# Means on VectorE and a reordered first split at the norms of a GLA and MLA decoder trunk

## The chip, the cores and the metric

The kernel runs on one core of one Trainium2 chip. The metric is the device time of one execution in microseconds (us), taken as the median over runs. Engines are named as in the profile: PE is TensorE (PEld its weight loads), DVE is VectorE, ACT is ScalarE, POOL is GpSimd, SP is SyncE, whose queue issues nearly all DMAs.

## The reference

Two decoder layers on x of 256 tokens by 2048 channels, in float32. Layer 0 is gated linear attention (GLA), layer 1 multi-head latent attention (MLA); each is followed by a gated MLP with a causal convolution of width 3. Every norm is an RMSNorm, modulated by a shift and a scale that come from the condition c; every residual is gated.

```python
def rmsnorm(x, g):
    xf = x.astype(jnp.float32)
    y = xf * lax.rsqrt(jnp.mean(xf * xf, axis=-1, keepdims=True) + EPS)
    return (y * g.astype(jnp.float32)).astype(x.dtype)

def modulate(h, shift, scale):
    return h * (1 + scale[:, None, :]) + shift[:, None, :]

# each layer:
    mod = c_act @ mod_w[i] + mod_b[i]          # 2048 by 12288 weights, six parts
    h = modulate(rmsnorm(x, norm_mix_g[i]), sh_m, sc_m)
    y = gla_mixer(h, ...) or mla_attention(h, ...)
    x = x + (1 + g_m)[:, None, :] * y
    h = modulate(rmsnorm(x, norm_ffn_g[i]), sh_f, sc_f)
    x = x + (1 + g_f)[:, None, :] * conv_ffn(h, w_up, conv_w, conv_b, w_down)
# at the end: rmsnorm(x, final_norm_g)
```

## The kernel before

**Weights as items.** All weight matrices are streamed as a numbered list of items of 4 row tiles by 512 columns (1 MB; the down projection of the last block group has 3 row tiles). SP loads item n into one of four buffers once PE has used item n-4. Float32 products are made from split numbers: ACT copies an item to its rounded high part (`hi`, L764), DVE subtracts to get the low part (`lo`, L1213), and PE multiplies high by high, high by low and low by high. `item` (L1893) has three orders: the plain one multiplies all high parts first (L1911, L1912) and the low parts last (L1918); the one with `turn` or `halves` (L1903 to L1905) needs the low part from its start. The last item of a section that ends in a norm has `halves`: the first 128 tokens are finished before the others. `AHEAD` is 3: ACT and DVE split item n+3 while PE multiplies item n.

**Modulation tiles.** The vector c times its 2048 by 2048 parts is made on DVE: one tile of 128 rows (1 MB) at a time is loaded into one of two buffers `mods` and gathered into `acc` (L1230). `MOD_PLACES` (L437) says at which item of which section each tile is gathered; SP issues its load three items ahead (L629 to L646), in the sections `gla_out` to `norm1` after the item's load, and waits for the gather of the tile two before (L551). A finished vector is summed over partitions by PE: `reduce_mod` (L1977) makes 16 products of one column for parts 4, 10 and 12 (L1990), and DVE adds the bias and makes the scale columns in `reduced` (L1276; L1293, L1295).

**A section before a norm.** `add_section` on DVE (L1382) handles the GLA output projection: per item it runs `lo`, the gather of `mods_at` and, for each finished chunk of 512 columns, gate times output plus x (L1350, L1351). `add_last` (L1353) does the last chunk in two token halves: L1357 and L1358 after the first half (`half_used`), L1360 and L1362 after the item (`item_used`). ACT squares each chunk and accumulates it along the row (L796), so that four partial sums for each of the two token tiles stand in `sq`. Here DVE gathers a modulation tile at items 3 to 14 of `gla_out`.

**The norm itself.** POOL's `boundary_root` (L698) adds the first three partial sums (L702, L703), and after the last squares the fourth (L705), makes mean plus epsilon (L706) and raises it to -0.5 (L707). While POOL does so, DVE makes the low part of item 14 + 3 of the section (L1395, L1733, L1872) and, before norm1 and norm5, the scale columns (`reduced(4)`, `reduced(12)`). Then DVE normalises the first two chunks (L1370), ACT the others later (L819). PE transposes xn in 8 fills of two channel tiles (16 fills at norm2, for two modulations), L1954, into the two banks of `tp`. Each fill is split: ACT makes the rounded modulated high part straight from the bank (L779), then DVE makes the modulated value (L1322) and subtracts (L1327). The first fill is handled tile by tile on DVE, so that PE can begin when the first tile's low part is there (`first_lo`, L2029). `turn_boundary` (DVE L1373, ACT L822) and `turn_two` (L1764, L844) hold this order; before fills 4 and 6 (at norm2 before every even fill from 4) DVE also makes the low parts of the next items.

The norms of this form are norm1 (after `gla_out`), norm2 (after `down02`), norm5 (after `mla_out`) and final. norm3 and norm4 are norms of the two latents, 512 wide; their sums come from ACT (L788) and their root from POOL (`root`, L688; L692 the mean, L693 the power). norm3's result is applied by DVE at fill 14 of norm2 (L1773), norm4's at L1789. At the end `scale_output(3)` (L1880, L1757) multiplies the last chunk by the final gain, and L1886 and L1194 apply the root.

Each engine executes its own instructions in order; they meet at semaphores.

Of the kernel before, what the change touches and what calls it, by code (L numbers as in the profile page):

```python
# [21 lines left out]
ALU = mybir.AluOpType  # L22
# [9 lines left out]
AHEAD = 3  # L32
# [104 lines left out]
def yoco_kernel(nc, x, c, positions, mod_w, mod_b, norm_mix_g, norm_ffn_g, gla_w_in, gla_w_gate2,  # L137
# [173 lines left out]
    with ExitStack() as ctx:  # L311
# [38 lines left out]
        half_used = sem("half_used")  # L350
        first_lo = sem("first_lo")
# [80 lines left out]
        def taken(m):  # L432
# [7 lines left out]
            ("gla_out", 4, 4, tuple(range(3, 15))),  # L440
# [25 lines left out]
        SUMS = {"norm0": 1, "norm3": 2, "norm4": 3}  # L466
        NORM = {"norm0": 0, "norm1": 1, "norm2": 2, "norm3": 3, "norm4": 4, "norm5": 5, "final": 6}
# [197 lines left out]
        def _(pool):  # L665
# [70 lines left out]
            boundary_root("norm1")  # L736
            boundary_root("norm2")
            norm_root("norm3", LAT)
            norm_root("norm4", LAT)
# [7 lines left out]
            boundary_root("norm5")  # L747
            boundary_root("final")
# [3 lines left out]
        def _(act):  # L752
# [19 lines left out]
            def split(fill, count, dst, scale, shift, from_=0):  # L772

                for f in range(count):
# [7 lines left out]
                    ins.then_inc(split_hi, 1)  # L782

# [38 lines left out]
            def turn_boundary(name, next_item, dst, scale, shift):  # L822

                s = a[name]
                for f in range(8):
# [4 lines left out]
                    split(s.tp + f, 1, dst, scale, shift, f)  # L830
# [13 lines left out]
            def turn_two(next_item):  # L844
# [3 lines left out]
                for f in range(16):  # L848
# [8 lines left out]
                    if f < 8:  # L857
                        split(s.tp + f, 1, (a_hi,), (kv,), (ab[:, A_OF["kv"] + 1],), f)
# [344 lines left out]
        def _(dve):  # L1203
# [102 lines left out]

            def split(name, count, dst, hi_of, scale, shift, from_=0, wrap=KT, both=both):

                fill = a[name].tp
                for f in range(from_, from_ + count):  # L1310

                    dve.wait_ge(split_hi, splits[name] + f + 1)
                    first = name in BOUND and f == 0
                    for ks in ((0,), (1,)) if first else ((0, 1),):
                        for m, (d, h_, sc_, sh_) in enumerate(zip(dst, hi_of, scale, shift)):
                            for k in ks:
                                kt = 2 * (f % wrap) + k
                                t = tp[:, (fill + f) % 2, k * T:(k + 1) * T]
                                if sh_ is None:
                                    ins = dve.tensor_scalar(both[:, k, :], t, sc_[:, kt:kt + 1], None, ALU.mult)  # L1320
                                else:
                                    ins = dve.tensor_scalar(both[:, k, :], t, sc_[:, kt:kt + 1],  # L1322
                                                            sh_[:, kt:kt + 1], ALU.mult, ALU.add)
                                v = step.mark(ins)
                            step.wait(v)
                            kts = slice(2 * (f % wrap) + ks[0], 2 * (f % wrap) + ks[-1] + 1)
                            ins = dve.tensor_tensor(d[:, kts, :], both[:, ks[0]:ks[-1] + 1, :],  # L1327
                                                    h_[:, kts, :].bitcast(F32), ALU.subtract)
# [44 lines left out]
            def turn_boundary(name, next_item, dst, hi_of, scale, shift):  # L1373
# [3 lines left out]
                for f in range(8):  # L1377
                    if f in (4, 6):
                        lo(next_item + f // 2)
# [1096 lines left out]
```

## Time and profile before

| | us |
|---|---|
| median of 3 runs | 2393.55 |
| lowest, highest | 2393.10, 2397.02 |
| the profiled execution: its time | 2393.17 |
| its span in the profile | 2391.2 |
| PE busy | 2308.2 |
| PEld busy | 1870.2 |
| DVE busy | 1847.2 |
| ACT busy | 1096.9 |
| POOL busy | 126.6 |

The span runs from the first to the last instruction of the profile; the execution's own time is 2.0 us longer. Busy times are of one engine each and overlap. A busy PE is not a PE at its peak: the mean granted clock was 0.982 of full speed, and it is below 1 just in a few stretches.

### The profile page before, as it was taken

To read this page: it belongs to the slowest core of one execution; us is meant where nothing else is said; L and a number is where in the kernel's file an instruction comes from. 1 tells how busy PE (TensorE), PEld (TensorE's weight loads), DVE (VectorE), ACT (ScalarE), POOL (GpSimd) and SP (SyncE) were. 2 spreads that over 40 slices of the span, in tenths; PEclk is the share of its full clock that TensorE was granted. 3 is DMA by queue.
4 is the path that set the end of the run, shared out by engine and by line. 5 is a ranking of instruction groups with operands and counts; after the bars stand their busy time and mean duration, and the time that the engine had idled before them with its cause. 6 is when DMAs were issued, how large, how long until landed. Compare 5 with 4: busy or idle time off the path is not lost.

```text
span 2391.2 us, 26862 instructions
## 1 busy us (share of the span) xinstructions
PE 2308.2 (97%) x10800; PEld 1870.2 (78%) x10800; DVE 1847.2 (77%) x1748; ACT 1096.9 (46%) x1192; POOL 126.6 (5%) x145
## 2 busy tenths in 40 slices
PE   5999999999999999999998999999999999999998
PEld 2478887778887888878887788877887888878886
DVE  5868997887998888888888777887777556564565
ACT  2244443544554354533554555435555345444454
POOL 0021740010000000000000000000000000000000
PEclk8999999999999999999999999999999999999999
DMA  9958789787997998889889475696776555555554
GB/s 363 383 198 293 250 300 351 250 315 268 348 325 275 359 336 304 291 303 370 323 281 330 130 224 187 253 340 218 274 270 223 193 194 178 190 177 193 193 180 154
DMA packets 259807, 632.89 MB, mean 265 GB/s; under 512 B 23505, under 2 KB 32745, under 8 KB 233978
## 3 DMA queue, kind: packets, MB, share of 16 engines
q1 hardware_dynamic: 258050, 625.90, 73.8%
q10 hardware_dynamic: 1656, 5.60, 0.6%
q8 instruction: 69, 1.13, 0.2%
q14 instruction: 32, 0.26, 0.0%
HBM read 629.36 MB, written 2.10 MB: 264 GB/s over the span
## 4 chain that ended last, share of the span: by engine, by line
PE 80%; DVE 8%; DMA 5%; issue 3%; ACT 2%; SPq 1%; POOL 1%; DVEq 0%; POOLq 0%; ACTq 0%
PE gm L1911 22%; PE gm L1912 22%; PE gm L1918 22%; PE tp L1954 2%; PE gm L1903 2%; DMA mods<-in_mod_w_dram 2%; PE gm L1905 2%; PE gm L1904 2%; DVE w_lo L1213 1%; DVE acc L1230 1%; DVE conv L1659 1%; DMA raw<-in_ffn_w_down_dram 1%; ACT w_hi L764 1%; PE ms L2064 1%; DMA raw<-in_gla_w_in_dram 1%
## 5 line engine op out<-in xcount | busy, mean ns | idle before, releaser
L1213 DVE TENSOR_TENSOR w_lo<-raw,w_hi 128x2048 fp32r<-128x2048 f32 (+1 forms) x378 | 851.9, 2255 | 330.2 <-ACT w_hi L764 328.5
L764 ACT ACTIVATE w_hi<-raw 128x2048 fp32r<-128x2048 f32 (+1 forms) x378 | 703.8, 1864 | 695.5 <-DMA raw<-in_ffn_w_up_dram 242.2
L1911 PE MATMUL gm<-w_hi,h_hi 128*128 128x512 f32 x1816 | 720.7, 397 | 1.6 <-DVE h_lo L1327 1.6
L1912 PE MATMUL gm<-w_hi,h_lo 128*128 128x512 f32 x1816 | 708.1, 390 | 0.0
L1918 PE MATMUL gm<-w_lo,h_hi 128*128 128x512 f32 x1816 | 448.7, 389 | 0.0
L1230 DVE SCALAR_TENSOR_TENSOR acc<-mods,c_col,acc 128x2048 f32<-128x2048 f32 x180 | 422.7, 2349 | 5.3 <-DMA mods<-in_mod_w_dram 4.8
L1911 PEld LDWEIGHTS gm<-w_hi,h_hi 128*128 128x128 f32 x1816 | 341.2, 188 | 77.9 <-issue 4.7
L1918 PEld LDWEIGHTS gm<-w_lo,h_hi 128*128 128x128 f32 x1816 | 340.9, 188 | 70.7
L1912 PEld LDWEIGHTS gm<-w_hi,h_lo 128*128 128x128 f32 x1816 | 341.3, 188 | 69.9 <-issue 1.7
L1911 PE MATMUL gm<-w_hi,a_hi 128*128 128x512 f32 x692 | 275.1, 398 | 11.6 <-DVE a_lo L1682 8.1
L1912 PE MATMUL gm<-w_hi,a_lo 128*128 128x512 f32 x692 | 271.2, 392 | 0.0
L1659 DVE SCALAR_TENSOR_TENSOR conv<-tp,cv_col,conv 128x255 f32<-128x255 f32 (+1 forms) x352 | 152.4, 477 | 76.9 <-ACT conv L1026 73.5
L1918 PE MATMUL gm<-w_lo,a_hi 128*128 128x512 f32 x692 | 173.4, 391 | 0.0
L1911 PEld LDWEIGHTS gm<-w_hi,a_hi 128*128 128x128 f32 x692 | 131.0, 189 | 43.6 <-DVE a_lo L1682 10.4
L1912 PEld LDWEIGHTS gm<-w_hi,a_lo 128*128 128x128 f32 x692 | 130.9, 189 | 28.4 <-issue 1.4
L1918 PEld LDWEIGHTS gm<-w_lo,a_hi 128*128 128x128 f32 x692 | 129.0, 188 | 26.2
L1026 ACT ACTIVATE conv<-tp,cv_col 128x256 f32<-128x256 f32 x176 | 88.4, 561 | 120.7 <-PE tp L1954 120.3
L770 ACT ACTIVATE u<-gm 128x1024 f32<-128x1024 f32 x76 | 77.5, 1020 | 133.3 <-PE gm L1918 129.6
L702 POOL TENSOR_TENSOR sq<-sq 128x2 f32<-128x2 f32 x4 | 5.3, 1329 | 1832.1 <-ACT tp L796 1832.1
L733 POOL TENSOR_TENSOR ex<-ex,qk_t 128x512 f32<-128x512 f32 x32 | 78.5, 2474 | 106.3 <-ACT ex L937 106.3
L1039 ACT ACTIVATE a_hi<-gated 128x256 f32 (+1 forms) x88 | 35.7, 417 | 85.7 <-DVE gated L1674 85.7
L779 ACT ACTIVATE h_hi<-tp,ab 128x256 fp32r<-128x256 f32 x64 | 32.0, 563 | 87.4 <-DVE ab L1445 50.9
(267 smaller groups left out, 2155.0 us busy)
## 6 DMA issues: line engine op xcount, KB each, us to landing
raw<-in_ffn_w_up_dram SPq DMA_DIRECT2D x176, 1024.0 KB, 5.1
mods<-in_mod_w_dram SPq DMA_DIRECT2D x170, 1024.0 KB, 7.1
raw<-in_ffn_w_down_dram SPq DMA_DIRECT2D x64, 1024.0 KB, 5.1
raw<-in_gla_w_in_dram SPq DMA_DIRECT2D x48, 1024.0 KB, 5.2
mods<-in_kv_mod_w_dram SPq DMA_DIRECT2D x32, 1024.0 KB, 7.0
raw<-in_ffn_w_down_dram SPq DMA_DIRECT2D x32, 768.0 KB, 4.4
raw<-in_gla_w_o_dram SPq DMA_DIRECT2D x16, 1024.0 KB, 7.1
raw<-in_mla_w_o_dram SPq DMA_DIRECT2D x16, 1024.0 KB, 5.6
```

Of the source, the lines that this page charges most:

```text
L733: pool.tensor_tensor(f, f, s, ALU.mult).then_inc(xq_made, 1)
L764: act.activation(w_hi[:, k % RAW, 0:words], raw[:, k % RAW, 0:words], ACT.Copy).then_inc(hi_made, 1)
L770: act.activation(dst, gm[:, par] if src is None else src, func).then_inc(u_made, 1)
L1026: ins = act.activation(conv[:, j % 2, side, :], tp[:, bank, side * T:(side + 1) * T], ACT.Identity, scale=cv_col[:, layer, 2, cs], bias=cv ...
L1213: dve.tensor_tensor(w_lo[:, k % RAW, 0:words], raw[:, k % RAW, 0:words], w_hi[:, k % RAW, 0:words].bitcast(F32), ALU.subtract).then_inc(lo ...
L1230: return dve.scalar_tensor_tensor(total, tile_, ck, total, ALU.mult, ALU.add)
L1659: ins = dve.scalar_tensor_tensor(v, tp[:, bank, side * T:(side + 1) * T - shift], cv_col[:, layer, tap, cs], v, ALU.mult, ALU.add)
L1903: pe.matmul(o, hi_s[:, kt, tok], wh[:, j, :], start=kt == 0, stop=False)
L1904: pe.matmul(o, hi_s[:, kt, tok], wl[:, j, :], start=False, stop=False)
L1911: pe.matmul(o, hi_s[:, kt, tok], wh[:, j, :], start=kt == 0, stop=False)
L1912: pe.matmul(o, lo_s[:, kt, tok], wh[:, j, :], start=False, stop=False)
L1918: return pe.matmul(o, hi_s[:, kt, tok], wl[:, j, :], start=False, stop=kt == total - 1)
```

## The change

Four things. The partial sums and the mean of norm1 to norm5 and final move from POOL to DVE: `add_last` adds the first three sums between its two halves, `boundary_root` and `latent_root` make mean plus epsilon, and POOL keeps only the power (`mean_root`). The first fill of norm1, norm2 and norm5 is split in another order: DVE makes the modulated value in `both`, ACT copies it to the rounded high part, DVE subtracts. The low part of the item that DVE made after `add_last` is now made before fill 2, and `reduced` comes after the normalising. The modulation tiles of `gla_out` are gathered (and loaded) one item earlier.

```diff
-            ("gla_out", 4, 4, tuple(range(3, 15))),
+            ("gla_out", 4, 4, tuple(range(2, 14))),
...
+        MEAN = {"norm1": 0, "norm2": 1, "norm3": 2, "norm4": 3, "norm5": 4, "final": 5}
...
-            def boundary_root(name):
-
-                done, dst = 8 * BOUND[name], TT * (NORM[name] % 2)
-                pool.wait_ge(sq_made, done + 6)
-                step.link(pool.tensor_tensor(sq[:, 4, :], sq[:, 0, :], sq[:, 1, :], ALU.add))
-                step.link(pool.tensor_tensor(sq[:, 4, :], sq[:, 4, :], sq[:, 2, :], ALU.add))
-                pool.wait_ge(sq_made, done + 8)
-                step.link(pool.tensor_tensor(sq[:, 5, :], sq[:, 4, :], sq[:, 3, :], ALU.add))
-                step.link(pool.tensor_scalar(sq[:, 5, :], sq[:, 5, :], 1.0 / D, EPS, ALU.mult, ALU.add))
+            def mean_root(name):
+
+                dst = TT * (NORM[name] % 2)
+                pool.wait_ge(mean_made, MEAN[name] + 1)
                 pool.tensor_tensor(stats[:, 1, dst:dst + TT], sq[:, 5, :], half_neg[:, 0:TT],
                                    ALU.pow).then_inc(rstd, 1)
...
+            def first_split(name, dst):
+
+                for k in range(2):
+                    act.wait_ge(both_made, 2 * BOUND[name] + k + 1)
+                    ins = act.activation(dst[:, k, :], both[:, k, :], ACT.Copy)
+                    ins.then_inc(first_hi if k == 0 else split_hi, 1)
...
+            def first_split(name, dst, hi_of, scale, shift):
+
+                fill = a[name].tp
+                dve.wait_ge(tp_done, fill + 1)
+                for k in range(2):
+                    dve.tensor_scalar(both[:, k, :], tp[:, fill % 2, k * T:(k + 1) * T], scale[:, k:k + 1],
+                                      shift[:, k:k + 1], ALU.mult, ALU.add).then_inc(both_made, 1)
+                dve.wait_ge(first_hi, BOUND[name] + 1)
+                dve.tensor_tensor(dst[:, 0, :], both[:, 0, :], hi_of[:, 0, :].bitcast(F32),
+                                  ALU.subtract).then_inc(first_lo, 1)
+                dve.wait_ge(split_hi, splits[name] + 1)
+                dve.tensor_tensor(dst[:, 1, :], both[:, 1, :], hi_of[:, 1, :].bitcast(F32),
+                                  ALU.subtract).then_inc(tp_free, 1)
+                dve.wait_ge(first_lo, BOUND[name] + 1)
+                dve.wait_ge(tp_free, fill + 1)
...
                 dve.tensor_tensor(x_sb[:, 0, cols], x_sb[:, 0, cols], u[:, 1, 0], ALU.add).then_inc(x_half, 1)
+                dve.wait_ge(sq_made, 8 * BOUND[after] + 6)
+                step.link(dve.tensor_tensor(sq[:, 4, :], sq[:, 0, :], sq[:, 1, :], ALU.add))
+                step.link(dve.tensor_tensor(sq[:, 4, :], sq[:, 4, :], sq[:, 2, :], ALU.add))
                 dve.wait_ge(item_used, a[name].item + 16)
...
+            def root(name, total, width):
+
+                dve.tensor_scalar(sq[:, 5, :], total, 1.0 / width, EPS, ALU.mult, ALU.add).then_inc(mean_made, 1)
+
+            def boundary_root(name):
+
+                dve.wait_ge(sq_made, 8 * BOUND[name] + 8)
+                step.link(dve.tensor_tensor(sq[:, 4, :], sq[:, 4, :], sq[:, 3, :], ALU.add))
+                root(name, sq[:, 4, :], D)
+
+            def latent_root(name):
+
+                dve.wait_ge(sums, TT * SUMS[name])
+                k = TT * (NORM[name] % 2)
+                root(name, stats[:, 0, k:k + TT], LAT)
...
-            def turn_boundary(name, next_item, dst, hi_of, scale, shift):
-
+            def turn_boundary(name, next_item, dst, hi_of, scale, shift, columns):
+
+                boundary_root(name)
                 dve.wait_ge(rstd, NORM[name] + 1)
                 normalise_chunks(name)
+                reduced(columns)
                 for f in range(8):
-                    if f in (4, 6):
+                    if f in (2, 4, 6):
                         lo(next_item + f // 2)
+                    if f == 0:
+                        first_split(name, dst[0], hi_of[0], scale[0], shift[0])
+                        continue
                     split(name, 1, dst, hi_of, scale, shift, f)
...
                 add_last(name, after)
-                lo(s.item + AHEAD + 14)
...
             def turn_two(next_item):
 
+                boundary_root("norm2")
                 dve.wait_ge(rstd, NORM["norm2"] + 1)
                 normalise_chunks("norm2")
...
-                    if f >= 4 and f % 2 == 0:
+                    if f >= 2 and f % 2 == 0:
                         lo(next_item + f // 2)
                     if f == 14:
+                        latent_root("norm3")
                         normalised("norm3", lat[:, 0], lat[:, 0], TT)
...
             lo(m.item)
+            latent_root("norm4")
             normalised("norm4", lat[:, 1], lat[:, 1], TT)
...
             add_last("mla_out", "norm5")
-            lo(s.item + AHEAD + 14)
-            reduced(12)
...
+            boundary_root("final")
             scale_output(3)
             dve.wait_ge(y_scaled, 4)
             dve.wait_ge(rstd, NORM["final"] + 1)
```

The general `split` on DVE loses its case for the first fill, and `down02` loses its `lo` after `add_last` in the same way as the other two.

## Rows read from the trace of the kernel before

**Rows 1.** The page, engines' shares of the chain that ended last:
```profile
PE 80%; DVE 8%; DMA 5%; issue 3%; ACT 2%; SPq 1%; POOL 1%; DVEq 0%; POOLq 0%; ACTq 0%
```

**Rows 2.** Waits of PE over the whole span: us in total, times, longest:
```profile
PE tp L1954 <- DVE xn L1370: 6.4, 3, 3.1
...
PE ms L1990 <- DVE acc L1230: 2.3, 1, 2.3
```

**Rows 3.** Timeline of DVE, end of `gla_out`: start, us, instruction, idle before:
```profile
521.21 2.34 DVE L1230 SCALAR_TENSOR_TENSOR acc<-mods,c_col,acc 128x2048 f32<-128x2048 f32 x1
525.22 2.35 DVE L1230 SCALAR_TENSOR_TENSOR acc<-mods,c_col,acc 128x2048 f32<-128x2048 f32 x1 [1.67 <-DMA mods<-in_mod_w_dram]
...
530.14 2.28 DVE L1213 TENSOR_TENSOR w_lo<-raw,w_hi 128x2048 fp32r<-128x2048 f32 x1
```

**Rows 4.** Timeline of ACT and POOL, the root of norm1:
```profile
530.79 0.19 ACT L796 ACTIVATION_READ_ACCUMULATOR tp<-x_sb 128x1 f32 x1
531.13 1.35 POOL L705 TENSOR_TENSOR sq<-sq 128x2 f32<-128x2 f32 x1 [7.53 <-ACT tp L796]
...
532.84 0.69 POOL L707 TENSOR_TENSOR stats<-sq,half_neg 128x2 f32<-128x2 f32 x1
```

**Rows 5.** The chain that ended last, in order of time, around norm1: start, us, what:
```profile
527.62 5.68 PE ms L1990 x32
...
533.75 0.89 DVE xn L1370 x2
...
534.89 1.10 PE tp L1954 x4
...
537.71 0.44 DVE h_lo L1327
...
538.19 0.79 PE gm L1903
```

**Rows 6.** Timelines of DVE and SP's queue, start of `gla_out`:
```profile
460.97 2.29 DVE L1213 TENSOR_TENSOR w_lo<-raw,w_hi 128x2048 fp32r<-128x2048 f32 x1 [2.58 <-ACT w_hi L764]
...
451.71 0.50 SPq L553 DMA_DIRECT2D mods<-in_mod_w_dram  x1
```

**Rows 7.** Stretches at norm1 and norm5: busy shares, then granted clock (PEclk), DMA:
```profile
542.00:543.00 1.00, 1.00 (x4) 0.76 (x4) 0.00 (x0) 0.99 (x2) 0.00 (x0) 0.63 0.00 0
...
1631.00:1632.00 1.00, 1.00 (x7) 0.96 (x6) 0.00 (x0) 0.09 (x1) 0.00 (x0) 0.70 0.00 0
```

**Rows 8.** Tiles `gated` and `stats`, small operations: duration min/median/max in ns:
```profile
L1039 ACT ACTIVATE a_hi<-gated x88: 401/418/423, 604.2 to 2329.6; 128x256 f32 x48, 128x256 fp32r<-128x256 f32 x40
...
L1827 DVE TENSOR_SCALAR stats<-stats x16: 169/170/170, 1423.0 to 1545.5; 128x2 f32<-128x2 f32 x16
```

**Rows 9.** Timelines of DVE at norm2 and norm5, and of PE at norm5:
```profile
1313.96 0.68 DVE L1360 TENSOR_TENSOR u<-gm,gate_b 128x512 f32<-128x512 f32 x1
...
1618.96 0.69 DVE L1360 TENSOR_TENSOR u<-gm,gate_b 128x512 f32<-128x512 f32 x1 [1.16 <-PE gm L1905]
...
1618.76 4.44 PE L1990 MATMUL ms<-ones,acc 128*128 128x1 f32 x32
...
1628.23 0.80 PE L1903 MATMUL gm<-w_hi,h_hi 128*128 128x512 f32 x1 [1.35 <-DVE h_lo L1327]
```

**Rows 10.** Timeline at fills 2 and 14 (DVE) and norm3's power (POOL):
```profile
543.13 0.99 DVE L1322 TENSOR_SCALAR both<-tp,ab 128x256 f32<-128x256 f32 x2 [2.33 <-ACT h_hi L779]
...
1367.78 0.88 DVE L1343 TENSOR_SCALAR lat<-lat,stats 128x512 f32<-128x512 f32 x2
...
1359.27 2.74 POOL L693 TENSOR_TENSOR stats<-stats,half_neg 128x2 f32<-128x2 f32 x1
```

**Rows 11.** Timeline of PE at fill 14, and of DVE and POOL at the end:
```profile
1370.43 0.47 PE L1903 MATMUL gm<-w_hi,h_hi 128*128 128x512 f32 x1
...
2381.01 1.23 DVE L1757 TENSOR_TENSOR y_out<-x_sb,mods 128x1024 f32<-128x1024 f32 x1
...
2381.80 0.49 POOL L705 TENSOR_TENSOR sq<-sq 128x2 f32<-128x2 f32 x1 [8.66 <-ACT tp L796]
```

More of the change, by code:

```diff
@@ L735, in _ @@
                 root(TT * h, TT, DV, o_sums, TT * (h + 1), o_rstd)
[L736 to L739, printed above, removed]
+            mean_root("norm1")
+            mean_root("norm2")
+            mean_root("norm3")
+            mean_root("norm4")
             pool.wait_ge(tp_free, at["norm4"].tp + 2)
@@ L746, in _ @@
                 step.mark(ins) if k == 0 else ins.then_inc(consts, 1)
-            boundary_root("norm5")
-            boundary_root("final")
+            mean_root("norm5")
+            mean_root("final")
         @block.scalar
@@ L829, in turn_boundary @@
                         hi(next_item + AHEAD)
-                    split(s.tp + f, 1, dst, scale, shift, f)
+                    if f == 0:
+                        first_split(name, dst[0])
+                    else:
+                        split(s.tp + f, 1, dst, scale, shift, f)
             def latent_out(side):
@@ L857, in turn_two @@
                     if f < 8:
-                        split(s.tp + f, 1, (a_hi,), (kv,), (ab[:, A_OF["kv"] + 1],), f)
+                        if f == 0:
+                            first_split("norm2", a_hi)
+                        else:
+                            split(s.tp + f, 1, (a_hi,), (kv,), (ab[:, A_OF["kv"] + 1],), f)
                     else:
@@ L1312, in split @@
                     dve.wait_ge(split_hi, splits[name] + f + 1)
[L1313 to L1328, printed above, removed]
-                            if m < len(dst) - 1:
-                                step.link(ins)
-                            elif first and ks == (0,):
-                                ins.then_inc(first_lo, 1)
-                            else:
-                                ins.then_inc(tp_free, 1)
@@ new lines, in split @@
+                    for m, (d, h_, sc_, sh_) in enumerate(zip(dst, hi_of, scale, shift)):
+                        for k in range(2):
+                            kt = 2 * (f % wrap) + k
+                            t = tp[:, (fill + f) % 2, k * T:(k + 1) * T]
+                            if sh_ is None:
+                                ins = dve.tensor_scalar(both[:, k, :], t, sc_[:, kt:kt + 1], None, ALU.mult)
+                            else:
+                                ins = dve.tensor_scalar(both[:, k, :], t, sc_[:, kt:kt + 1],
+                                                        sh_[:, kt:kt + 1], ALU.mult, ALU.add)
+                            v = step.mark(ins)
+                        step.wait(v)
+                        kts = slice(2 * (f % wrap), 2 * (f % wrap) + 2)
+                        ins = dve.tensor_tensor(d[:, kts, :], both[:, :, :], h_[:, kts, :].bitcast(F32), ALU.subtract)
+                        if m < len(dst) - 1:
+                            step.link(ins)
+                        else:
+                            ins.then_inc(tp_free, 1)
@@ L1644, in _ @@
             add_section("gla_out", "norm1")
[L1645 removed]
             turn_boundary("norm1", a["up00"].item, (h_lo,), (h_hi,), (ab[:, A_OF["ffn0"]],),
[L1647 removed]
+                          (ab[:, A_OF["ffn0"] + 1],), 4)
             def conv_tile(layer, g, blk, j, fill, tile_):
```

14 lines of the change are left out of this document (9 added, 5 removed).

## The prediction

> **What bounds the kernel now.** I read the chain that ended last, then PE's waits, then the timelines of each stretch that the diff touches. In the chain PE holds 80% of the span, DVE 8% and POOL 1% [rows 1]. So almost everywhere a step off PE costs nothing, and the change can only act where PE stands still. The waits name these places: 6.4 us in three waits for xn, which are norm1, norm2 and norm5, and 2.3 us before the reduction of part 4 [rows 2]. Around each norm PE has no work until the first low part is there: at norm1 its item ends at 527.62 - 2.33 = 525.3, and its next large product starts at 538.19 [rows 2, 5]. I follow that stretch backwards, because each instruction in it is one that the change moves.
>
> At norm1 DVE is late before the norm starts. Its gather of item 13 ends at 523.55, and then it waits 1.67 us for the last tile, gathers until 527.57 and only then begins with the last chunk [rows 3]. PE's reduction also waits for that gather and takes 5.68 us [rows 5]. After the last squares (530.98) POOL needs until 533.53 [rows 4]. Of this the fourth addition takes 1.35 us on two numbers a partition. It ends at 532.48, and DVE's low part of a whole item (530.14 + 2.28) ends at 532.42 [rows 3, 4]. At the end of the kernel it is the same again: DVE's product ends at 2382.24, POOL's addition, 0.49 us this time, at 2382.29 [rows 11]. So POOL stands until DVE's operation on two SBUF tiles is over. A page of the Trainium skill, "SBUF — State Buffer", section "Who interferes with whom", says so: DVE instructions with two SBUF inputs exclude a GpSimd instruction that reads SBUF, and the first to issue keeps the port. By that rule, the trace agrees.
>
> **Gathers one item earlier.** DVE's idle 2.58 us before item 3's low part [rows 6] takes the extra gather (2.34 us) at item 2. Its tile comes early enough: the first load was issued at 451.71, after item 6's load; one item earlier it goes out at about 445, some 13 us before its gather at 458.4, and SP passes the next weight load no later, since the gather of two tiles before is long done. From item 3 on all gathers stand where they stood, and the one at item 14 is gone. The cover for this is that 2.58 us; without it DVE would be 2.3 us late on low parts that PE does not wait for in that section. So L1357 starts at 523.6 instead of at about 527.5. Its two operations and the two new sums (0.17 us each by the small DVE operation [rows 8], 0.21 with the link) end at 525.4, when PE's item has just ended. L1360 and L1362 then end at 526.85, and the squares at 527.6 instead of 530.98: **3.4 us**.
>
> **The mean on DVE, the lo moved.** From the end of the squares to the start of xn POOL took 2.58 us (2.77 at norm1 with `reduced` behind it) [rows 4, 5]. After: 0.06 handoff, 0.21 sum, 0.17 mean, 0.06 handoff, 0.69 power [rows 4, 8], 0.03 handoff = 1.22 us. DVE has nothing running meanwhile, so POOL does not stand. That is **1.4 us** at each of norm1, norm2 and norm5. At norm1 xn starts at 528.8, and PE can transpose 1.14 us later, at 529.95, as it did after 533.75 [rows 5]. PE must also have finished the reduction, which now starts at 525.3. It took 4.44 us at norm5, right behind full work [rows 9], and 5.68 us here, so it ends between 529.7 and 531.0. I take the 4.44, since it will be as at norm5; the upper bound costs 1.0 us. `reduced` behind xn ends at 530.9, before the transposes of the first fill (531.1), so it costs nothing; with a 5.68 us reduction it would also end before its fill does.
>
> The additions inside `add_last` are free where DVE waits for PE after L1358, as at norm5 (1.16 us idle). At norm2 L1360 followed without idle time [rows 9], so there they cost **0.4 us**. They wait for the third chunk's squares, which end before L1358 does at all four norms; behind that wait stands the last chunk.
>
> The moved low part (2.28 us) falls before fill 2, where DVE was idle for 2.33 us [rows 10]. PE wants that item only after 24 products of the first one, over 8 us after its start, so I cost it at nothing; without cover it is 2.2 us a norm.
>
> **The first split.** From the transposes' end (534.89 + 1.10) to PE's product it took 2.20 us [rows 5]. After: 0.06 handoff, 0.54 the modulated value (0.99 for two [rows 10]), 0.03, ACT's copy 0.42 [rows 8], 0.03, subtraction 0.44 [rows 5], 0.05 = 1.57 us. The second value (done 0.99 after the start) and the second copy lie beside. **0.6 us** at each of three norms. The copy reads SBUF in the row and here alike.
>
> **norm3 and norm4.** Before, POOL had norm3's root ready by 1362.0, long before DVE used it at 1367.78 [rows 10]. Now DVE makes the mean at that place and waits: 0.17 + 0.06 + 0.69 + 0.04 = 0.96 us. What is queued behind is fill 14's low part, and PE waited for just that: its product stands at 1370.43, right behind it [rows 11]. So this **costs 1.0 us**, the whole of it. At norm4 the mean stands behind a low part for which PE waits and ahead of nothing that PE waits for, so nothing.
>
> **The end.** `boundary_root("final")` stands before `scale_output(3)`, which used to run (2381.01) while ACT squared [rows 11]. Now DVE waits for the squares until 2381.7, makes sum and mean until 2382.1 and starts the 1.23 us product 0.03 us later, ahead of POOL, which the handoff delays by 0.06. POOL stands until 2383.35; norm3's power shows what follows: it started under a DVE low part, took 2.74 us and ended 0.55 us after that was over [rows 10]. So the root comes at 2383.9 instead of 2383.35: **0.5 us lost**. If POOL were not held, the product would end at 2383.35 and nothing would be lost. The same section of "SBUF — State Buffer" in the Trainium skill gives the port to whoever issues first; had POOL been first, by its 0.69 us the product would end at about 2384.1, 0.7 us lost.
>
> **The sum.** norm1: 538.19 - (529.95 + 1.14 + 1.57) = 5.5 us. norm2: 1.4 + 0.6 - 0.4 = 1.6. norm5: 1.4 + 0.6 = 2.0; its squares end 2.2 us after L1360's start as at norm1, at 1621.1, so the transposes can start at 1621.1 + 1.22 + 1.14 = 1623.5, and the reduction is over at 1623.2 [rows 9]. Less 1.0 (norm3) and 0.5 (end): 7.6 us. Against the profiled execution (2393.17) this is 2385.6; the median of the runs shown is 0.4 us above it, so **2386.0 us**. What comes later keeps the gain, because loads and splits are paced by the items that PE has used.
>
> The clock is the term that I set at zero. PE's clock is at 1.2 GHz when it starts after a norm (granted 0.50) and returned to 2.4 GHz at 542.7, 4.5 us after the first product, and at norm5 at 1631.6, 3.4 us after it (1628.23) [rows 5, 7, 9]; where in its slice it returned follows from the slice's mean, 0.63 and 0.70. At half the clock each us costs about 0.5. I assume that the return moves with the start. If it comes 1.1 us earlier or later, as these two rows differ, at all three norms, that is 1.7 us either way.
>
> **The rivals.** (a) The clock's return does not move with the start. Then half of the 9.1 us by which the starts move is lost at the lower clock: 4.6 - 1.5 = 3.1 us gained, **2390.5**. For it: in the rows the return does not stand at a fixed distance from the start. (b) The last tile of part 4 is late all the same, for its load is paced by gathers, not by items (it waited 1.67 us [rows 3]). Then norm1 gains just 1.8 us: 3.9 us in all, **2389.7**. Against it: the load of item 13's tile came in time before, with one more tile behind it. (c) The moved low part delays fill 2 at three norms: 3 x 2.2 lost, 1.0 us gained, **2392.6**. Against it stands DVE's idle time of that length. (d) Slower: POOL's long first operations are a start after idle time and do not come from DVE's operation beside them. Then the power, now POOL's only operation, meets it each time. At 2.74 us [rows 10] it costs 2.05 more at norm1, norm2, norm3, norm5 and final: 10.3 lost against 7.6, **2396.2**. It turns the sign when the power takes over 0.69 + 1.5 = 2.2 us at each. Against it: the two ends within 0.06 us of DVE's, and the 0.69 us of the powers with DVE idle. (e) That the gathers do not move or the root still waits for POOL's sums is excluded by the diff.
>
> **How the numbers follow.** Forecast 0.76, (a) 0.09, (b) 0.06, (c) 0.05, (d) 0.04. A measurement can tell 0.2% (4.8 us) from no change. Faster by more: nearly all of the forecast, 0.75. Within: the rest of it, (a) to (c) and most of (d), 0.22. Slower by more: 0.03. The range: at the low end the clock gives 1.7 us, the end loses nothing (0.5), and 0.3 is left for the handoffs, 2386.0 - 2.5 = 2383.5; at the top it reaches (a) with its 2390.5, which also holds the forecast less 1.0 for the longer reduction and 1.7 for the clock.
>
> **What would show it.** Right: L1357 of norm1 at about 523.6 without a gather before it; 1.2 us from the squares' end to xn; powers of 0.69 us, except one of 1.7 at the end; first products after the norms 5.5, 1.6 and 2.0 us sooner after their section's last product; a PE wait of 1 us at fill 14. Wrong: a power above 1 us at norm1, norm2 or norm5; idle PE before item 1 of `up00` or `latent`; a clock that returns over 6 us after the first product; PE waiting in `gla_out` for low parts.

## The result and the profile after

The changed kernel took 2382.31 us in the median of 5 executions (2379.17 to 2385.29) against 2393.1 for the kernel before (5 executions): ratio 0.9947, interval 0.9934 to 0.9959. The profiled execution took 2379.23 us with a span of 2377.1. The forecast was 2386.0 with a range from 2383.5, so the direction was right and the gain came out larger than the range allowed.

At norm1 the order of the steps is the predicted one. In the chain that ended last, around norm1 of the changed kernel (start, us, what):

```profile
520.25 2.35 DVE acc L1242
522.60 0.61 DVE u L1380
...
524.23 0.70 DVE u L1386
...
526.43 0.17 DVE sq L1397
...
526.63 0.18 DVE sq L1392
...
526.88 0.70 POOL stats L706
...
527.60 0.89 DVE xn L1412 x2
...
528.74 1.10 PE tp L2003 x4
...
529.94 0.55 DVE both L1324
...
530.58 0.42 ACT h_hi L787
...
531.03 0.44 DVE h_lo L1327
...
531.51 0.79 PE gm L1952
```

The last gather is followed by the last chunk without a wait [rows 3 had 1.67 us]. From the last square (526.41) to xn (527.60) it is 1.19 us, where the prediction had 1.22. From the transposes' end (529.84) to the product (531.51) it is 1.67, for 1.57. What is not the predicted one is where the last chunk lies against PE (PE's timeline):

```profile
522.89 4.61 PE L2039 MATMUL ms<-ones,acc 128*128 128x1 f32 x32
```

PE's item ends at 522.89, where the reduction begins without a wait. The first half of the chunk (L1380) starts 0.4 us before that, where the prediction had 1.7 (523.6 against 525.3), and the second half (L1386) 1.34 us after it, where the prediction had 0.1 (525.4). So the gap that the prediction saw after the change was 7.8 us (13.3 less 5.5), and this profile has 8.9.

The PE waits of the same profile (us in total, times, longest) show the three waits for xn at 4.3 us instead of 6.4 [rows 2]:

```profile
PE tp L2003 <- DVE xn L1412: 4.3, 3, 2.2
```

POOL's power over the whole run (ns min/median/max):

```profile
L706 POOL TENSOR_TENSOR stats<-sq,half_neg x6: 690/691/1612, 526.9 to 2367.7; 128x2 f32<-128x2 f32 x6
```

Five take 0.69 us, norm3's among them (2.74 before [rows 10]). The long one is at the end, in the timeline of the end (start, us, instruction, idle before):

```profile
2367.44 0.17 DVE L1392 TENSOR_SCALAR sq<-sq 128x2 f32<-128x2 f32 x1
2367.52 1.22 DVE L1801 TENSOR_TENSOR y_out<-x_sb,mods 128x1024 f32<-128x1024 f32 x1
2367.69 1.61 POOL L706 TENSOR_TENSOR stats<-sq,half_neg 128x2 f32<-128x2 f32 x1 [758.34 <-DVE sq L1392]
```

DVE's product is issued first and ends at 2368.74, the power 0.56 us after that. At norm3 and fill 14 the cost stands where it was forecast (timelines of POOL, DVE and PE):

```profile
1354.59 0.69 POOL L706 TENSOR_TENSOR stats<-sq,half_neg 128x2 f32<-128x2 f32 x1 [48.20 <-DVE sq L1392]
1355.32 0.88 DVE L1366 TENSOR_SCALAR lat<-lat,stats 128x512 f32<-128x512 f32 x2 [0.81 <-POOL stats L706]
...
1357.98 0.47 PE L1952 MATMUL gm<-w_hi,h_hi 128*128 128x512 f32 x1 [0.97 <-DVE h_lo L1353]
```

So in these two profiles the single steps have nearly their sizes, norm1 as a whole gains 4.4 us for 5.5, and together they do not give 10.8 us. Matching the two traces product by product gives 14.1 us of span: 4.4 at norm1, 1.5 at norm2, 1.2 at norm5, less 1.0 and 0.5; the other 8.4 us came in stretches that the change does not touch. One is a clock fall. From 1018 to 1030 us the granted clock was 0.72 in the kernel before and 1.00 in its repeat (first `before`, then r1_before; stretch, PE, PEld, DVE, ACT, POOL busy, then granted clock, DMA share, GB/s):

```profile
1018.00:1030.00 12.00, 9.29 (x32) 7.21 (x31) 6.06 (x7) 2.58 (x4) 0.00 (x0) 0.72 0.49 175
```
```profile
1018.00:1030.00 12.00, 10.15 (x47) 8.41 (x48) 6.06 (x8) 5.38 (x5) 0.00 (x0) 1.00 0.73 268
```

Where the rest of the 8.4 us came from is not shown. Two theories follow: (A) the change is worth its own terms, the rest is the chance of few executions; (B) the 10.8 us are its lasting worth. Repeats and part changes had to tell them apart.

### The profile page after: what moved, and what is told of

Read it like the earlier page. It is cut to its first block, busy times and chain, and to the rows that moved or that the text cites. A ratio compares the mean times of both kernels' runs of the same rounds, so it can differ in the third digit from the quotient of the medians.

```text
span 2377.1 us, 26862 instructions
## 1 busy us (share of the span) xinstructions
PE 2301.8 (97%) x10800; PEld 1865.5 (78%) x10800; DVE 1849.8 (78%) x1766; ACT 1096.3 (46%) x1192; POOL 111.3 (5%) x127
## 4 chain that ended last, share of the span: by engine, by line
PE 49%; issue 34%; DVE 8%; DMA 5%; ACT 2%; SPq 1%; POOL 0%; POOLq 0%; DVEq 0%; ACTq 0%
PE gm L1960 12%; PE gm L1961 12%; PE gm L1967 12%; DVE acc L1242 2%; PE tp L2003 2%; DVE w_lo L1225 2%; DMA mods<-in_mod_w_dram 1%; PE gm L1952 1%; ACT w_hi L763 1%; PE gm L1954 1%; PE gm L1953 1%; PE ms L2113 1%; DMA raw<-in_ffn_w_down_dram 1%; PE ms L2247 1%; DMA raw<-in_mla_w_o_dram 1%
## 5 line engine op out<-in xcount | busy, mean ns | idle before, releaser
L1960 PEld LDWEIGHTS gm<-w_hi,a_hi 128*128 128x128 f32 x692 | 129.9, 188 | 42.9 <-DVE a_lo L1727 10.3
L706 POOL TENSOR_TENSOR stats<-sq,half_neg 128x2 f32<-128x2 f32 x6 | 5.1, 844 | 1919.7 <-DVE sq L1392 1919.7
```

What stands on the lines that cost most here:

```text
L1960: pe.matmul(o, hi_s[:, kt, tok], wh[:, j, :], start=kt == 0, stop=False)
```

## The experiments

The yardstick is the gap: from the start of the section's last product to the start of the first product after the norm (at norm1 of the kernel before 524.90 to 538.19, of the changed one 522.66 to 531.51). Loads and clock outside it do not touch it; a clock that falls inside it does. The last column runs from the start of the last product of all to the end of the span.

| profile of | norm1 | norm2 | norm5 | end |
|---|---|---|---|---|
| before | 13.3 | 10.3 | 9.7 | 12.1 |
| r1_before | 15.6 | 9.6 | 9.7 | 12.2 |
| r3_before | 17.1 | 9.6 | 9.7 | 12.1 |
| after | 8.9 | 8.8 | 8.5 | 12.6 |
| r2_after | 9.8 | 7.8 | 7.6 | 12.6 |
| e6_after_again | 8.0 | 9.3 | 7.8 | 12.6 |
| r4_after | 8.6 | 7.7 | 7.8 | 12.6 |
| e11_after_third | 9.5 | 7.7 | 8.5 | 12.6 |
| e1_only_gather | 10.1 | 9.6 | 9.7 | 12.1 |
| e9_gather_again | 9.7 | 9.8 | 9.7 | 12.1 |
| e2_no_gather | 12.2 | 8.4 | 7.4 | 12.6 |
| e7_only_lo | 16.6 | 8.5 | 9.1 | 12.1 |
| e8_only_split | 16.9 | 9.0 | 9.1 | 12.1 |
| e3_mean3_early | 8.7 | 8.1 | 7.4 | 12.6 |
| e4_root_late | 8.4 | 9.2 | 7.8 | 12.1 |
| e5_both | 8.7 | 9.7 | 7.8 | 12.1 |
| e10_both_again | 8.2 | 7.7 | 7.5 | 12.2 |

### The kernel before, again

No edit.

> The kernel before once more, unchanged, for a second profile and more times. Theory A (own steps): the change itself gains what the three gaps around norm1, norm2 and norm5 show, 4.4 + 1.5 + 1.2 us, less 1.0 at norm3 and 0.5 at the end, 5.6 us together; the other 8 us between the two profiles come from stalls outside the changed code at which the clock happened to fall in one execution and not in the other. Then this profile lies anywhere between 2388 and 2397, and its clock falls at other places than 1020.6 and 1433.6. Theory B (the rest is systematic): the stalls near 1020 and 1433 lower the clock in every execution of this kernel; then both low stretches, 6.8 and 3.4 us long, are here again.

Measured: 2389.76 us, ratio 0.9999 (0.9983 to 1.0014). Both theories miss here: the profiled execution took 2384.65 us, below theory A's 2388, and from 1018 to 1030 and from 1425 to 1445 us its granted clock was 1.00, where theory B wanted both low stretches again.

> The kernel before once more, for a third profile of it and one more session. Theory C (each term is near its size, but the kernel before varies more than the changed one, because its last tile at norm1 comes at a time that its load sets): the gap from the last product of gla_out to the first of up00 is anywhere from 13 to 17 us, against 8.0 to 9.8 in the changed kernel's three profiles; the gaps at norm2 and norm5 are 9.6 to 10.3 and 9.7 us; no stretch between the norms is longer than in the changed kernel by more than clock falls and landings explain. Rival D (something between the norms is lastingly slower in the kernel before): one such stretch is over 2 us longer with the same clock.

Measured: 2393.89 us, ratio 1.0004 (0.9993 to 1.0014). The gap at norm1 is 13.3, 15.6 and 17.1 us in the three profiles of one and the same kernel, with norm2 and norm5 alike. Theory C holds and D falls: its stretches between the norms are 772.0, 298.1 and 754.4 us long, the changed kernel's (r4_after, same session) 774.6, 299.4 and 753.1. The timelines of DVE and PE in r3_before show where the time is:

```profile
524.92 2.35 DVE L1230 SCALAR_TENSOR_TENSOR acc<-mods,c_col,acc 128x2048 f32<-128x2048 f32 x1 [2.63 <-DMA mods<-in_mod_w_dram]
...
527.33 1.01 PE L1990 MATMUL ms<-ones,acc 128*128 128x1 f32 x4 [4.83 <-DVE acc L1230]
```

and its stretches (columns as above):

```profile
527.30:534.30 7.00, 6.97 (x32) 6.90 (x32) 4.76 (x5) 3.25 (x5) 2.23 (x3) 0.50 0.21 82
534.30:538.00 3.70, 1.95 (x9) 1.57 (x8) 2.02 (x6) 0.88 (x2) 0.00 (x0) 0.50 0.00 0
```

The last tile came 2.63 us late, not 1.67, and the last gather began 2.4 us after PE's item had ended (527.33 - 4.83 = 522.50). In the profile that the prediction was read from it began 0.1 us before that (525.22 against 525.29). PE stood for 4.83 us instead of 2.33 [rows 2], and the reduction then ran wholly at 1.2 GHz: 7 us instead of 5.68 [rows 5].

In r1_before the last gather began 0.9 us after PE's item had ended (524.94 - 3.30 = 521.64):

```profile
522.53 2.35 DVE L1230 SCALAR_TENSOR_TENSOR acc<-mods,c_col,acc 128x2048 f32<-128x2048 f32 x1 [2.67 <-DMA mods<-in_mod_w_dram]
...
524.94 6.99 PE L1990 MATMUL ms<-ones,acc 128*128 128x1 f32 x32 [3.30 <-DVE acc L1230]
```

The issue of that tile's load, on SP's queue in `before`, r1_before and r3_before, says what differs:

```profile
519.11 0.34 SPq L553 DMA_DIRECT2D mods<-in_mod_w_dram  x1
```
```profile
515.10 0.34 SPq L553 DMA_DIRECT2D mods<-in_mod_w_dram  x1
```
```profile
517.85 0.34 SPq L553 DMA_DIRECT2D mods<-in_mod_w_dram  x1
```

Each time it goes out within 0.03 us of the end of the gather of item 12, which frees the buffer. From there to the last gather it is 6.1, 7.4 and 7.1 us, so this transfer was about 1 us quicker in the profile that the prediction was read from. And the issue came 6.2, 6.5 and 4.7 us before PE's item ended: in r3_before DVE itself was 1.5 us further behind PE.

### The changed kernel, again

No edit.

> The changed kernel once more. Theory A: low clock stretches may appear near 1012 and 1423, and the gain over the kernel before comes nearer to 5.6 us, a time of about 2387. Theory B: no low stretch there again, and a time within 2 us of 2381.

Measured: 2385.39 us, ratio 0.9976 (0.9964 to 0.9989), nearer to theory A's 2387 than to theory B's 2381. From 1418 to 1432 us its clock was low (granted 0.76).

> The changed kernel once more, in a third session. Theory A (own terms 5.6 us, the rest chance): a ratio of 0.9970 to 0.9985, as the 0.9976 of the second session. Theory B: a ratio of 0.9955 or less, as the 0.9947 of the first.

Measured: 2381.42 us, ratio 0.9948 (0.9928 to 0.9968): theory A missed, theory B's band met.

> The changed kernel once more, beside the kernel before of the same session. Theory C: in the mean 7 to 9 us less than the kernel before; ratio 0.9962 to 0.9972, and a smaller scatter than the kernel before has. Theory B (10.8 us and more is the change's lasting worth): 0.9955 or less.

Measured: 2385.12 us, ratio 0.9961 (0.9947 to 0.9974), just below C's band. The smaller scatter that C expected is not shown: all 42 executions of the changed kernel scatter by 3.4 us (standard deviation), 143 of the kernel before by 3.8.

> The changed kernel beside these two. Theory C: 8 to 9 us less than the kernel before (7.2 at norm1, 1.1 at norm2, 2.0 at norm5, less 1.0 at norm3 and 0.5 at the end), ratio 0.9962 to 0.9967; the gap at norm1 8 to 10 us, with at most 0.5 us of wait for the last tile.

Measured: 2383.21 us, ratio 0.9962 (0.9946 to 0.9977), as C expected.

In the means of the five sessions the change gained 11.2, 6.7, 12.6, 7.6 and 8.5 us; weighted by the executions of the changed kernel (5, 12, 6, 7, 12) that is 8.8 us (2392.8 to 2384.1). The gains of 6.7 and 12.6 us have standard errors of 1.2 and 1.6 us, so the sessions differ by somewhat more than their scatter explains. Each ran on another chip, as far as recorded (the first is not); what makes them differ stays open. If each execution counts alike, the 8.8 us have an error of 0.7, and neither A's 5.6 nor B's 10.8 stands. If each session counts alike, the gain is 9.3 with an error of 1.1: A still falls, B is not ruled out by the times. Against B stand the terms themselves, which add up to less.

### The gathers alone, and all but the gathers

```diff
# e1_only_gather, e9_gather_again: the kernel before with
-            ("gla_out", 4, 4, tuple(range(3, 15))),
+            ("gla_out", 4, 4, tuple(range(2, 14))),
# e2_no_gather: the changed kernel with
-            ("gla_out", 4, 4, tuple(range(2, 14))),
+            ("gla_out", 4, 4, tuple(range(3, 15))),
```

> The kernel before with the gathers of gla_out at items 2 to 13 and nothing else. Own steps: DVE begins the last chunk at about 523.5, the squares end 3.4 us sooner, the root follows at 2.58 us, xn at 530.3 instead of 533.75, and norm1's gap shrinks by about 3.2 us; 0.13% faster, about 2390. If the gap at norm1 does not shrink, the reduction of part 4 or the scale columns behind it bound it, and the time stays within 1 us of before.

Measured: 2388.42 us, ratio 0.9984 (0.9971 to 0.9998). The gap at norm1 is 10.1 us, the expected 3.2 less than in the profile of `before`.

> The kernel before with the gathers of part 4 one item earlier, once more. Theory C (the norm1 term was too small because the profile it was read from had an early last tile; without a gather at item 14 that lateness is gone, and with it the slow reduction behind it): no wait of DVE for the last tile, a reduction of at most 5.4 us, the gap at norm1 10 to 11 us against the 13.3, 15.6 and 17.1 us of the kernel before, so 5 to 6 us of gain from this one part where the prediction had 3.4 with the reduction's 1.2; norm2 and norm5 as before, 9.6 and 9.7 us. In the time 4 to 6 us, ratio 0.9975 to 0.9985. Rival E (the tile is late one item earlier as well, in some executions): a DVE wait of 1 us or more before the last gather, and a gap of 12 us or more.

Measured: 2387.78 us, ratio 0.9984 (0.9970 to 0.9997). The gap is 9.7 us, even under the 10 expected. Its PE timeline at the reduction and its stretch:

```profile
521.02 3.64 PE L1990 MATMUL ms<-ones,acc 128*128 128x1 f32 x32
```
```profile
521.10:524.60 3.50, 3.50 (x33) 3.47 (x31) 3.35 (x3) 1.93 (x3) 1.06 (x1) 0.98 0.60 190
```

PE did not stand before the reduction, kept its 2.4 GHz (granted 0.98) and took 3.64 us. Rival E falls: neither profile has a DVE wait there. With 15.3 us as the mean of the three gaps before, this part alone is worth 5.4 us at norm1 (15.3 to the mean of 10.1 and 9.7); the forecast had 3.4.

> The changed kernel with the gathers back at items 3 to 14. Own steps: norm1's gap is about 3 us longer than in the changed kernel, everything else as there: about 2385. If the gathers explain none of it, within 1 us of the changed kernel.

Measured: 2389.30 us, ratio 0.9991 (0.9977 to 1.0005), 4 us over the expected 2385. The gap at norm1 is 12.2 us, 3.2 over the mean of the changed kernel, so from this side the gathers are worth 3.2 us and from e1 and e9 5.4; each rests on one or two profiles. The late tile is back, with all the rest of the change in place (DVE's timeline):

```profile
523.10 2.35 DVE L1242 SCALAR_TENSOR_TENSOR acc<-mods,c_col,acc 128x2048 f32<-128x2048 f32 x1 [2.78 <-DMA mods<-in_mod_w_dram]
```

### The moved low part alone

```diff
 # turn_boundary
-                    if f in (4, 6):
+                    if f in (2, 4, 6):
                         lo(next_item + f // 2)
 # turn_two
-                    if f >= 4 and f % 2 == 0:
+                    if f >= 2 and f % 2 == 0:
 # behind add_last, twice
-                lo(s.item + AHEAD + 14)
```

> The kernel before, with one edit: the low part of the next section's first item goes from ahead of the norm to ahead of fill 2. POOL still makes the sums, the mean and the power. Theory A (POOL's fourth addition took 1.35 us because DVE's operation on two SBUF tiles held the port): that addition takes 0.2 us at norm1, norm2 and norm5, from the last square to xn it is 1.4 to 1.5 us rather than 2.6, and the gaps at norm2 and norm5 are 1.1 us shorter, 8.7 and 8.6 us; at norm1 the 5 to 7 us reduction still stands ahead of xn, so less is gained there. Rival (the sums on POOL are slow by themselves, for POOL has stood for hundreds of us): the addition stays at 1.3 us and the gaps at 9.7 us. If theory A holds, moving the mean to DVE as such is worth under 0.4 us a norm.

Measured: 2390.74 us, ratio 0.9987 (0.9975 to 0.9999). POOL's fourth addition, all four norms (ns min/median/max):

```profile
L705 POOL TENSOR_TENSOR sq<-sq x4: 194/194/484, 529.7 to 2381.8; 128x2 f32<-128x2 f32 x4
```

The addition falls from 1.35 [rows 4] to 0.19 us at the three norms, and stays at 0.48 at the end [rows 11], where DVE's product on two SBUF tiles still runs. A start after idle time, rival (d), is no cost. Norm2 gained the 1.1 us. Norm5 gained 0.6 only, for what was late next (timeline of ACT, POOL and DVE):

```profile
1621.10 0.19 ACT L796 ACTIVATION_READ_ACCUMULATOR tp<-x_sb 128x1 f32 x1
...
1621.98 0.69 POOL L707 TENSOR_TENSOR stats<-sq,half_neg 128x2 f32<-128x2 f32 x1
...
1622.89 0.17 DVE L1293 TENSOR_TENSOR modc<-ms,pcol 128x16 f32<-128x16 f32 x1 [2.36 <-PE ms L1987]
...
1623.30 1.67 DVE L1370 TENSOR_SCALAR xn<-x_sb,stats 128x512 f32<-128x512 f32 x4
```

The power ended at 1622.67, but `reduced` stood ahead of xn and waited for PE's reduction. That is what moving `reduced` behind xn is for; the prediction had counted its worth without naming it.

This run also says what the first of the four changes is worth. From the last square (1621.29) to the end of the power it is 1.38 us here, with sums and mean still on POOL, and 1.17 us in the changed kernel (526.41 to 527.58). So of the 1.4 us that the prediction gives to "the mean on DVE, the lo moved" about 1.2 come from the moved low part, and 0.2 from the mean on DVE. By the prediction's own terms the same move costs 0.4 us at norm2 and, where its wait was placed badly, 1.0 at norm3 and 0.5 at the end. The change without it was not run.

### The first split alone

```diff
+                    if f == 0:
+                        first_split(name, dst[0], hi_of[0], scale[0], shift[0])
+                        continue
                     split(name, 1, dst, hi_of, scale, shift, f)
```

and the same in `turn_two` and on ACT.

> The kernel before, with one edit: the first split goes from DVE to ACT to DVE. Theory A: from the end of the first fill's transposes to the first product 1.6 us rather than 2.2, so gaps 0.6 us shorter at each of norm1, norm2 and norm5 (9.1 us at norm5). Rival (the copy on ACT comes no sooner than the copy from PSUM did, and two handoffs are added): 2.1 us or more, gaps as before.

Measured: 2389.17 us, ratio 0.9989 (0.9977 to 1.0001). The gap at norm5 is 9.1 us, at norm2 9.0. In the timeline at norm5 the product starts 2.69 us after the first transpose does (1619.62 to 1622.31), where it was 3.30 at norm1 of the kernel before (534.89 to 538.19 [rows 5]), so 0.6 us less, as forecast. The time of the whole run (an interval that holds 1) shows nothing by itself:

```profile
1619.62 1.94 PE L1991 MATMUL tp<-ident,xn 128*128 128x128 f32 x8 [2.57 <-DVE xn L1401]
...
1620.75 0.99 DVE L1327 TENSOR_SCALAR both<-tp,ab 128x256 f32<-128x256 f32 x2 [0.59 <-PE tp L1991]
...
1622.31 0.80 PE L1940 MATMUL gm<-w_hi,h_hi 128*128 128x512 f32 x1 [0.75 <-DVE h_lo L1330]
```

### Mending the two losses

```diff
 # e3_mean3_early: the changed kernel with
-                    if f == 14:
+                    if f == 13:
                         latent_root("norm3")
+                    if f == 14:
 # e4_root_late: the changed kernel with
-            boundary_root("final")
             scale_output(3)
+            boundary_root("final")
 # e5_both, e10_both_again: both
```

> After, with norm3's mean moved from ahead of fill 14's low part to ahead of fill 13's. Theory A (the change is worth what its own terms add up to, norm3's mean costing 1.0 us because fill 14's low part stands behind DVE's wait for the power): the power runs beside a low part of fill 13, PE's wait at fill 14 of about 1 us goes away unless the mean's inputs are not there yet, and the time between the last product of norm2's side and fill 14's product is 0.9 to 1.0 us shorter. The power may then take up to 2.7 us beside DVE's operation without harm. Rival (the 0.96 us at norm3 came from something else, a load or the clock): the stretch between norm2 and norm5 keeps its length and PE waits as before. Whole time: 1 us less than after, not to be told from it by the median.

Measured: 2383.11 us, ratio 0.9953 (0.9935 to 0.9971). In the timeline at fill 14 neither DVE nor PE waits any more, and matched product by product the trace gains 1.00 us at that place. The power ran at fill 13, where DVE had no low part beside it, and took 0.69 us:

```profile
1356.12 0.87 DVE L1366 TENSOR_SCALAR lat<-lat,stats 128x512 f32<-128x512 f32 x2
...
1358.77 0.47 PE L1953 MATMUL gm<-w_hi,h_hi 128*128 128x512 f32 x1
```

> After, with the last tile's product with the scale put ahead of the final norm's sum and mean, as it was before the change. Theory A (at the end POOL's power is held by DVE's product on two SBUF tiles): the product starts about 0.9 us sooner, as before the change, and ends before the power can start; the power takes 0.69 us, not 1.61, and the stretch from PE's last product to the end is 0.4 to 1.0 us shorter than after's 12.59 us. Rival (the power at the end is slow because POOL had done nothing for 758 us): the power takes 1.6 us with DVE idle as well and the stretch stays at 12.5 us or grows.

Measured: 2383.71 us, ratio 0.9958 (0.9943 to 0.9974). The end in this kernel's timeline:

```profile
2372.45 1.23 DVE L1801 TENSOR_TENSOR y_out<-x_sb,mods 128x1024 f32<-128x1024 f32 x1
...
2374.03 0.69 POOL L706 TENSOR_TENSOR stats<-sq,half_neg 128x2 f32<-128x2 f32 x1 [761.10 <-DVE sq L1392]
```

After 761 us of idle time the power takes 0.69 us once DVE is quiet; the stretch at the end is 12.12 us, not 12.59.

> Both edits together, the version meant to beat the two kernels. Theory A: 1.0 us at norm3 and 0.4 to 1.0 us at the end on top of after, so 7 to 8 us less than the kernel before in the mean of undisturbed places, a ratio of 0.9970 with an interval that takes in after's. Theory B (the 10.8 us of the first comparison is a lasting property of the change, not of five executions): a ratio of 0.9945 or less.

Measured: 2382.75 us, ratio 0.9954 (0.9937 to 0.9971), between the two theories, with theory A's 0.9970 just inside the interval. Beside it the changed kernel (e6_after_again) had 2381.42 us, 1.3 us less.

> The changed kernel with norm3's mean ahead of fill 13 and the final root behind the last product, once more. From the terms measured so far (1.0 us at norm3, 0.46 us at the end) 1.5 us less than the changed kernel beside it, 10 us less than the kernel before, ratio 0.9955 to 0.9962. Rival F (the scatter of the executions is not chance but the mended kernel has lost something elsewhere): no less than the changed kernel, and a stretch in its profile that is longer by 1 us or more.

Measured: 2382.39 us, ratio 0.9965 (0.9950 to 0.9980), against the changed kernel's 2383.21 in the same session: 0.8 us less, and a ratio just above the expected band. Over all executions the mended kernel averages 2382.6 (18) and the changed one 2384.1 (42). That is the 1.5 us of the two terms, but no comparison in one session tells the two kernels apart, so the mended one is better by its traces and not shown better by its time. It beats the kernel before. Rival F is not borne out: the stretches of e10_both_again are 773.9, 293.5 and 751.3 us, those of e11_after_third 772.7, 295.9 and 751.3. The first is 1.2 us longer, just over F's mark, but the three together are shorter, and over the five profiles of the changed kernel the first runs from 769.8 to 774.6.

## Why the prediction was right or wrong

**The steps that held.** The mean on DVE (1.19 us from square to xn, for 1.22), the first split (0.6 us, e8), the hold of POOL by DVE (e7), the free `reduced` and low part (no PE wait at fill 2 or item 1), norm3's 1.0 us (0.97; e3) and the end's 0.5 (0.46; e4). Of the root's 1.4 us most belongs to the moved low part (e7). The rule of the Trainium skill in "SBUF — State Buffer", section "Who interferes with whom", by which a DVE instruction with two SBUF inputs keeps POOL's reads out and the first to issue keeps the port, is borne out by the two power times, 1.61 us behind the product and 0.69 without it. In these rows DVE issued first each time; the other order, GpSimd first, no run here shows. Norm2 gave 1.6 us (9.8 to 8.3 in the means) as forecast. In the changed kernel it swings between 7.7 and 9.3 with DVE's lag: where DVE has caught up, as in r4_after, it waits 1.09 us for PE before L1386, and where it has not, L1386 follows the sums at once and each added sum is paid. Norm5 gave 1.7 (9.7 to 8.0) for 2.0. There is a bound that the prediction saw at norm1 and norm5 only: where the clock falls within the reduction, it takes 4.8 instead of 3.6 us, and in r4_after at norm2 and norm5 and in e11_after_third at norm2 the transposes start as it ends.

**The step that failed** is the term of norm1, 5.5 us, whose first part, "Gathers one item earlier", was worked out from one execution (530.98 - 527.6 = 3.4 us). (The expectation of e9 books 1.2 us for the reduction beside it; the sum of the prediction has no such term.) Its mechanism is right and its size is off, at both ends. Before the change the gap was taken as 13.3 us, and the mean of three profiles is 15.3. In the profile that was read, DVE's last gather began as PE's item ended. In the two repeats it began 0.9 and 2.4 us after it: in r1_before because the tile took 1.3 us longer to come, in r3_before because it took 1.0 us longer and DVE was 1.5 us later. The reduction behind the longer standstill took 7.0 instead of 5.7 us. After the change the gap was to be 7.8 us, and the mean of five profiles is 8.9. The last chunk was to start 1.7 us before PE's item ended; it starts between 1.2 us before and 0.4 us after it. So the two added sums, free by the prediction at norm1, are paid there in `after`.

Norm1 is worth 15.3 - 8.9 = 6.4 us in the means of the profiles, not 5.5; with the gaps of e7 and of e8 (0.6 added for its split) among those before, the mean of five is 16.0 and norm1 7.1. Three of these five, r3_before, e7 and e8, come from one session, and they are the three in which DVE was late as well as the tile; the 7.1 may lean on that session. So the sum is 6.4 (7.1) + 1.6 + 1.7 - 1.0 - 0.5 = 8.2 (8.9) us, where 8.8 was measured. That the lateness belongs to the gather at item 14 is shown from both sides, by e9 and e2. Why the transfer takes 6.1 us in one execution and 7.0 to 7.8 in five others, and why DVE was late in those three, was not tried.

**The range failed for another reason as well**, and without it the time would have lain inside. A gain of 8.8 us from 2393.1 is 2384.3, which the range holds; the other 2 us of the first measurement are the chance of five executions, or of that session. The range held the bounds of the terms but not the scatter of the measurement. A kernel whose executions lie between 2376.9 and 2390.7 us gives medians of few executions that differ by some us: 2382.3, 2385.4, 2381.4, 2385.1 and 2383.2 in the five sessions. A low end of 2381 would have cost nothing. The clock, set to zero, was rightly so at the three returns, in the mean: after the first products it stays low for 4.6, 4.6 and 3.4 us in `before` and for 4.0, 3.5 and 4.3 in `after`, and over all profiles of the two kernels for 4.3 and 4.5 us. A single return lies anywhere between 2.9 and 6.1 us in the one and 3.2 and 5.9 us in the other, so the 1.1 us that the prediction took from two rows was too narrow for one norm. Inside the reductions the clock did count: it made the 7.0 us at norm1 before the change and the 4.8 us named above.

**The rivals.** (a) would have given less than the forecast, and its condition, a return that does not move, is not seen. (b) has its reason right, since the load is issued as the gather two tiles before ends, but not its cost: in the changed kernel the last tile makes DVE wait 0.47 us in one profile of five (r2_after, whose gap is the longest, 9.8 us) and not at all in four. (c) falls: behind the first product PE waits for nothing that the moved low part delays, in any of the five. (d) falls with the power's 0.69 us after idle times of 48 and 761 us.

## What to carry to other kernels

A wait for a transfer is the term of a sum that varies most from one execution to the next: before sizing an edit that removes it, look at it in more than one profile, and count what stands behind it, here a reduction that ran at half the clock after PE had stood. When a change moves several things, ask for each what it is worth alone: here the moved low part had nearly all the gain that was booked to the moved mean. A tiny instruction on the way to a root belongs where no operation on two SBUF tiles runs beside it, and before the point at which its consumer wants the result. Give the range the scatter of the median, not of the model alone.

## What the runs showed of the hardware

The same 32 one-column products of the reduction took 3.6 us behind full work where the granted clock stayed up (e9: 3.64, granted 0.98) and 3.9 to 4.9 us where it fell within them (granted 0.91 to 0.72). Behind a standstill of PE they took 5.35 us after 0.51 us of it (r2_after, granted 0.67), 5.68 after 2.33 (0.63), and 7 after 3.30 and after 4.83 us (0.50 throughout).

A GpSimd operation on two numbers a partition costs 0.19 us (addition) or 0.69 us (power), the power even after 761 us of idle time. Issued behind a DVE operation on two SBUF tiles, the power ended 0.56 us after that operation and the addition 0.06 us after it.
